# A two-layer encoder step on one core: one phase for load and index projection, feed-forward credits given early, level correction and masks inside the first attention

## The chip, the cores and the metric

The kernel runs on one core of a Trainium2 chip. The metric is the time of one execution in device microseconds (us), as the median of several runs. Before the change it is 3289.69 us (three runs, 3287.46 to 3293.42). The engines are called PE (TensorE, matmul), ACT (ScalarE), DVE (VectorE), POOL (GpSimd) and SP (SyncE, which issues all DMAs here).

## The reference

One inference step over 1024 prompt tokens and 32 sample tokens of width 1024, all in float32. Layer 0 has sparse attention: an index projection gives 8 heads of index queries, one index key and 8 weights per token; their relu scores choose, for each query, the 256 best keys (40 for a sample query), and 16 heads attend to those alone.

```python
dots  = einsum('bthd,bsd->bths', qi, ki)
score = einsum('bths,bth->bts', relu(dots), wi * IDX_SCALE)
score = where(key_pos < chunk_limit(q_pos), score, -inf)
_, sel = top_k(score, n_sel)                 # then softmax attention on k[sel], v[sel], with ALiBi
```

Layer 1 has differential attention. Behind each token mixer stand a residual with layer norm, and then

```python
ffn = (silu(x @ w_gate13) * (x @ w_up13)) @ w2
ple = sigmoid(x @ w_gate) * (p @ w_ple)
y   = layer_norm(ALPHA * x + ffn + ple, g, b)
```

## The kernel before

The program is written by hand, engine by engine. Each phase is a function that returns five streams of instructions, for SP, POOL, PE, ACT and DVE; the streams of all phases are strung together, and semaphores order them. PE, ACT and DVE each go through a barrier (`phase_over`) at the end of some phases; SP and POOL have none and run ahead as far as their own waits let them. Nothing but the written order decides what an engine does next.

Every float32 product of the projections is made of three matmuls: activations are kept as `x_hi` and `x_lo`, weights as `w_hi` and `w_lo`, and hi·hi, lo·hi and hi·lo are added in PSUM. A weight unit is 1024 by 128 (eight 128 by 128 blocks, 512 KB). SP loads it into a slot of a ring (`load_unit`), POOL makes hi and lo of it (`split_unit`, L121 and L123), and PE multiplies it by three pieces of 352 tokens (`unit_product`, L152), 24 matmuls per piece.

**Load (`load_x`, L171).** Eight token tiles of 128 rows come through a buffer of two tiles, `x_nat`. SP loads a tile, PE transposes it in eight blocks (L223), ACT copies each half bank to `x_hi` (L243), DVE subtracts for `x_lo` (L261), and when the transposes of a tile are done SP loads the next into its place. The 32 sample tokens come last (L228). Then DVE makes the row of parameters (L267, L269), the table of distances (L273) and lambda (L278 to L284), and a barrier ends the phase. The weights of the index projection are issued by SP behind all tiles (L107).

**Index projection (`index_projection`, L294).** Five units, 15 pieces; ACT copies each piece out of PSUM (L347, L350); DVE copies the keys (L360); PE transposes keys and weights back to rows (L339); DVE copies these (L362 to L364) and SP stores them. The barrier at the end also waits until that store has landed.

**First attention (`mixer_a`, L374).** It scores all query tiles. Then a search by bits finds for tiles 2 to 7 the level that leaves 256 keys: 31 rounds of counting, tiles 2 to 5 on DVE (L828), tiles 6 and 7 on ACT (L735), while PE works through the projections of q, k and v. Behind the search DVE corrects the levels of tiles 6 and 7 (L848 to L862, two counts at L854), makes the mask of tile 2 in eight operations (`masking`, L874 to L902), and then starts the attention. The attention has 72 steps, eight (two heads each) per query tile, tile 0 first and the sample tile last. In step g PE transposes probabilities of step g-2 (L594), makes the logits of step g (L579), and multiplies for step g-2 (L613); DVE copies a group of transposed probabilities (L943), reads the logits of two heads with the mask added (L929), and scales outputs at every second step (L950, L952); ACT does the exponentials. After the second read of a step DVE does one piece of the mask of the tile that comes three tiles later:

```python
            if g % 8 == 0 and g < STEPS:
                t = g // 8
                later = masking(t + 3) if t + 3 < QT else mask_sample() if t + 3 == SAMPLE else None
```

**Feed-forward (`ffn_norm`, L1755), once per layer.** First the per-layer embedding: eight times a gate (ACT, sigmoid, L2164) and a product, which DVE multiplies into the gate (L2267) and adds with both halves of x into `o_col` (L2270, L2273). Then a loop over pairs of blocks: gate (PE L152, ACT silu L2183), up (DVE L2286), down (L2033, DVE L2257). The waits inside that loop are written as if a round had gone before; so each engine adds credits to its own semaphore once (`s_si` 3, `s_h` 3, `s_hl` 3, `s_da` 24). In the kernel before, ACT gives `s_si` after the last addition of the embedding (L2176, behind a wait on `s_acc`), and DVE gives the others behind its own last instruction of the embedding (L2275 to L2277). PE waits ahead of the loop for the last product into the gate (`s_t`), and in it for `s_da` and `s_si`.

## Time and profile before

| | |
|---|---|
| median of three runs | 3289.69 us |
| the profiled execution | 3293.85 us |
| its span (first to last instruction) | 3292.1 us |
| PE busy | 3108.2 us (94%) |
| PE weight load, DVE, ACT, POOL busy | 2902.7, 1554.4, 887.2, 1021.8 us |
| granted TensorE clock, mean | 0.964 |
| DMA, mean over the span | 45 GB/s |

A matmul row of the timeline gives start and length in us; a group row gives the start of its first instruction. In brackets stand the idle time of the engine before the row and what ended it. PEclk is the granted clock of TensorE as a share of 2.4 GHz: 1.00 is 2.4 GHz, 0.50 is 1.2 GHz. Matmuls are pipelined, so that the time between two starts is shorter than the length of one.

### The profile page before, as it was taken

The page shows a single profiled execution, that of the slowest core. Times are in us where ns is not written, and L with a number is a line of the kernel's source. Part 1 is how long each engine was busy: PE and PEld are TensorE (multiplying, and loading weights), DVE is VectorE, ACT ScalarE, POOL GpSimd, SP SyncE. Part 2 cuts the span into 40 slices and gives each one's busy share as a digit, 9 for nine tenths or more (in the row PEclk, how much of TensorE's full clock was granted, in tenths as well). Part 3 has the DMA queues.
Part 4 walks back from the last instruction along what each step waited for, and adds up shares of the span by engine and source line. Part 5 has one row for each costly group of instructions (what it writes and reads, how often), then busy time and mean ns, then how long its engine had stood idle before and what let it go on. Part 6 is the DMA issues. An engine that isn't in the chain of part 4 may idle for free.

```text
span 3292.1 us, 49272 instructions
## 1 busy us (share of the span) xinstructions
PE 3108.2 (94%) x19621; PEld 2902.7 (88%) x19621; DVE 1554.4 (47%) x2889; ACT 887.2 (27%) x1921; POOL 1021.8 (31%) x495
## 2 busy tenths in 40 slices
PE   7897899989989999999999999998998999999996
PEld 7587677777989999999988999976798999999996
DVE  2589675444544333343363555565454433334335
ACT  2356354434110011100133445454401011110112
POOL 2123000024543343333333222212445343333432
PEclk8998599989999999999999999998999999999998
DMA  2121000012221111111012111111222111111101
GB/s 84 32 53 52 0 1 1 1 52 65 66 83 45 38 51 45 50 45 38 26 46 70 49 42 48 49 40 58 65 85 59 45 45 51 45 45 45 45 7 53
DMA packets 209371, 149.73 MB, mean 45 GB/s; under 512 B 28914, under 2 KB 195764, under 8 KB 209236
## 3 DMA queue, kind: packets, MB, share of 16 engines
q1 hardware_dynamic: 209236, 147.85, 15.1%
q8 instruction: 95, 1.56, 0.2%
q14 instruction: 40, 0.33, 0.0%
HBM read 128.09 MB, written 19.73 MB: 45 GB/s over the span
## 4 chain that ended last, share of the span: by engine, by line
PE 88%; DVE 6%; issue 2%; ACT 2%; POOL 1%; DMA 1%; POOLq 0%; SPq 0%; ACTq 0%; DVEq 0%
PE psum L152 48%; PE psum L2033 15%; PE psum L1637 6%; PE psum L613 5%; PE psum L579 3%; PE psum L594 3%; DVE junk L828 2%; PE psum L1225 2%; PE psum L1199 2%; PE psum L1213 1%; PE psum L534 1%; PE psum L548 1%; PE psum L1174 0%; PE psum L1591 0%; DMA x_nat<-in_x_prompt_dram 0%
## 5 line engine op out<-in xcount | busy, mean ns | idle before, releaser
L152 PE MATMUL psum<-x_hi,w_hi 128*128 128x352 f32 (+1 forms) x3192 | 1041.4, 326 | 40.1 <-ACTq L2176 23.2
L152 PE MATMUL psum<-x_lo,w_hi 128*128 128x352 f32 (+1 forms) x3192 | 1028.0, 322 | 0.0
L152 PE MATMUL psum<-x_hi,w_lo 128*128 128x352 f32 (+1 forms) x3192 | 1027.9, 322 | 0.0
L121 POOL TENSOR_TENSOR w_hi<-w_raw,zeros 128x1024 fp32r<-128x1024 f32 (+1 forms) x209 | 381.9, 1827 | 1549.6 <-PE psum L152 957.8
L152 PEld LDWEIGHTS psum<-x_hi,w_hi 128*128 128x128 f32 (+1 forms) x3192 | 601.7, 189 | 42.8 <-ACTq L2176 23.8
L152 PEld LDWEIGHTS psum<-x_lo,w_hi 128*128 128x128 f32 (+1 forms) x3192 | 602.8, 189 | 0.5
L152 PEld LDWEIGHTS psum<-x_hi,w_lo 128*128 128x128 f32 (+1 forms) x3192 | 601.5, 188 | 0.5
L123 POOL TENSOR_TENSOR w_lo<-w_raw,w_hi 128x1024 fp32r<-128x1024 f32 (+1 forms) x209 | 491.8, 2353 | 16.4
L2286 DVE TENSOR_TENSOR gate<-psum,gate 128x352 f32<-128x352 f32 x120 | 63.0, 525 | 756.9 <-PE psum L152 756.9
L2033 PE MATMUL psum<-h_hi,w_hi 128*128 128x352 f32 x1056 | 340.8, 323 | 1.3 <-DVE h_lo L2308 1.0
L2033 PE MATMUL psum<-h_lo,w_hi 128*128 128x352 f32 x1056 | 338.3, 320 | 0.0
L2033 PE MATMUL psum<-h_hi,w_lo 128*128 128x352 f32 x1056 | 338.1, 320 | 0.0
L2257 DVE TENSOR_TENSOR o_col<-psum,o_col 128x352 f32<-128x352 f32 x528 | 263.3, 520 | 157.4 <-PE psum L2033 155.2
L2033 PEld LDWEIGHTS psum<-h_hi,w_hi 128*128 128x128 f32 x1056 | 198.0, 188 | 2.0 <-issue 1.6
L2033 PEld LDWEIGHTS psum<-h_lo,w_hi 128*128 128x128 f32 x1056 | 198.3, 188 | 0.0
L2033 PEld LDWEIGHTS psum<-h_hi,w_lo 128*128 128x128 f32 x1056 | 197.9, 187 | 0.0
L2290 DVE TENSOR_TENSOR h_lo<-gate,h_hi 128x352 fp32r<-128x352 f32 x120 | 197.3, 1670 | 0.0
L613 PEld LDWEIGHTS psum<-valsA,ptA 128*128 128x128 f32 (+1 forms) x1216 | 154.3, 199 | 40.1 <-issue 25.6
L2186 ACT ACTIVATE h_hi<-gate 128x352 fp32r<-128x352 f32 x120 | 59.8, 498 | 426.9 <-DVE gate L2286 426.9
L613 PE MATMUL psum<-valsA,ptA 128*128 128x65 f32 (+1 forms) x1216 | 172.9, 288 | 0.9 <-ACT ptA L699 0.4
L2183 ACT ACT_TABLE_LOAD x20 | 25.7, 1283 | 499.3 <-PE psum L152 499.3
L1410 DVE CUSTOM_DVE_ANT_0 probB<-psum,distB 128x128 f32<-128x128 f32 (+5 forms) x144 | 96.4, 707 | 121.0 <-PE psum L1199 120.0
(465 smaller groups left out, 4157.0 us busy)
## 6 DMA issues: line engine op xcount, KB each, us to landing
w_raw<-in_ffn_w_dram SPq DMA_DIRECT2D x132, 512.0 KB
w_raw<-in_b_w_in_dram SPq DMA_DIRECT2D x24, 512.0 KB
w_raw<-in_ple_w_gate_dram SPq DMA_DIRECT2D x16, 512.0 KB
x_nat<-in_x_prompt_dram SPq DMA_DIRECT2D x8, 512.0 KB, 3.8
w_raw<-in_a_w_in_dram SPq DMA_DIRECT2D x8, 512.0 KB
w_raw<-in_a_w_in_dram SPq DMA_DIRECT2D x16, 256.0 KB
x_rows<-x_rows SPq DMA_DIRECT2D x8, 512.0 KB, 2.6
out_new_b_v_prompt_dram<-valsB SPq DMA_DIRECT2D x8, 512.0 KB, 3.4
```

What stands on the lines that cost most here:

```text
L121: nc.gpsimd.tensor_tensor(c.w_hi[s][:, 0:kc], c.w_raw[s][:, 0:kc], zero, ALU.add).then_inc(c.split[s], 1)
L123: nc.gpsimd.tensor_tensor(c.w_lo[s][:, 0:kc], c.w_raw[s][:, 0:kc], c.w_hi[s][:, 0:kc].bitcast(F32), ALU.subtract).then_inc(c.split[s], 1)
L152: last = c.nc.tensor.matmul(out, w, x, start=(n == 0), stop=(n == 3 * len(terms) - 1))
L579: mm = nc.tensor.matmul(c.psum[0:n, 1024 * m + a:1024 * m + a + size], queries[rows, 4 * c2 + 2 * i + j, q:q + n], keys[rows, c2, key:key ...
L594: mm = nc.tensor.transpose(bank(c, 4 + k % 2)[0:size, P * x:P * x + n], prob[0:n, g % 3, m, key:key + size], c.ident[0:n, 0:n])
L613: mm = nc.tensor.matmul(c.psum[0:n, at:at + 65], pt[0:size, k, x, 0:n], vals[0:size, blk, 2 * c2 + m, :], start=(j == 0 and x == 0), stop= ...
L828: nc.vector.tensor_scalar(junk[t][:, :], score(t), level[:, t - 2:t - 1], 0.0, ALU.is_ge, ALU.add, accum_out=count[:, t - 2:t - 1]).then_i ...
L1410: nc.vector.tensor_tensor_reduce(prob[:, sl, m, 0:L], c.psum[:, 1024 * m:1024 * m + L], dist[:, o:o + L], slope(h), -LOWEST, ALU.add, ALU.min,
L1637: mm = nc.tensor.matmul(out, o[t % 2][:, u, 0:n], ww[:, cols], start=(j == 0 and x == 0), stop=(j == KC - 1 and x == 2))
L2033: mm = nc.tensor.matmul(o, w[s][:, m, :], h[:, j, piece(t)], start=(j == 0 and k == 0), stop=(j == 1 and k == 2))
L2257: nc.vector.tensor_tensor(o, src, o, ALU.add).then_inc(s_da, 1)
L2290: nc.vector.tensor_tensor(h_lo[:, j, piece(done)], gate[:, 1, piece(done)], h_hi[:, j, piece(done)].bitcast(F32), ALU.subtract).then_inc(s ...
```

## The change

There are three parts.

1. `load_x` and `index_projection` become one phase, `load_index`. All nine token tiles have a place of their own, so SP issues every load without waiting: tiles 0 to 2, weight unit 0, tiles 3 to 5, unit 1, tiles 6 to 8, the parameters, then the other units. PE transposes tiles 0 to 3, multiplies piece 0 of unit 0, transposes tiles 4 and 5, multiplies piece 1, transposes tiles 6 to 8, multiplies piece 2, and goes on with the twelve pieces of units 1 to 4. There is no barrier between the two halves. The parameters are transposed behind the last piece, and DVE copies them there.
2. In `ffn_norm` the credits are given at the start of ACT's and DVE's streams.
3. In `mixer_a` the correction of the levels (`settle`) and the mask of tile 2 move behind the first reads of the attention. The mask of tile t is made during tile t-2, where it was t-3, and two pieces go behind each step, where it was one; `settle` follows the mask of tile 4, in tile 2. Its counts write to `tie`, no longer to `junk`.

```diff
-def load_x(c):
...
+def load_index(c):
+    nat = c.at("x_nat", [P, QT + 1, D], F32, 0)
...
+    GROUP = (0, 1, 1, 2, 2, 2, 3, 3, 3)
+    RING = (4, 5, 6, 7)
...
+    def half_bank(t, b):
+        n = rows(t)
+        return bank(c, RING[(2 * t + b) % 4], 4 * n).rearrange("p (k t) -> p k t", k=4)
...
+        x_tile(0)
+        x_tile(1)
+        x_tile(2)
+        weights(0)
+        for t in (3, 4, 5):
+            x_tile(t)
+        weights(1)
+        for t in (6, 7, 8):
+            x_tile(t)
...
+        def turn_x(t):
+            n = rows(t)
+            pe.wait_ge(s_x[GROUP[t]], 16 * GROUP.count(GROUP[t]))
+            for b in (0, 1):
+                if t >= 2:
+                    pe.wait_ge(s_lo, 2 * t + b - 3)
+                for k in range(4):
+                    mm = nc.tensor.transpose(half_bank(t, b)[:, k], nat[0:n, t, P * (4 * b + k):P * (4 * b + k) + P],
+                                             c.ident[0:n, 0:n])
+                mm.then_inc(s_t, 1)
...
+            if u == 0:
+                pe.wait_ge(s_lo, (6, 12, 18)[t])
...
+        for t in range(4):
+            turn_x(t)
+        project(0, 0)
+        turn_x(4)
+        turn_x(5)
+        project(0, 1)
+        for t in (6, 7, 8):
+            turn_x(t)
+        project(0, 2)
+        for u in range(1, 5):
             for t in range(PIECES):
...
+                project(u, t)
+        pe.wait_ge(s_par, 80)
+        nc.tensor.transpose(bank(c, 6)[:, 0:66], par[:, :], c.ident[0:66, 0:66]).then_inc(s_t, 1)
         pe.wait_ge(s_ca, 16)
         pe.wait_ge(s_q, 12)
         nc.tensor.transpose(c.psum[0:64, 512 * 3:512 * 3 + P], cache[:, :], c.ident[:, :]).then_inc(s_nt, 1)
         pe.wait_ge(s_kw, 3)
+        pe.wait_ge(s_lo, 19)
...
     def vector(v):
...
+        v.wait_ge(s_t, 19)
+        nc.vector.tensor_copy(c.params[:, :], bank(c, 6, 66)).then_inc(s_lo, 1)
+        v.wait_ge(s_lo, 19)
+        nc.vector.tensor_scalar(c.rms_gain[:, :], c.params[:, 64:65], 1.0 - LAMBDA_INIT, None,
+                                ALU.mult).then_inc(s_lo, 1)
         for t in range(PIECES):
             v.wait_ge(s_kw, t + 1)
...
+        def settle():
+            nonlocal masks
+            a = slice(ND, 6)
+            v.wait_ge(s_mask, masks)
+            nc.vector.tensor_scalar(above[:, a], level[:, a], 1.25 * 2.0 ** -24, None, ALU.mult).then_inc(s_mask, 1)
...
+            for t in ON_ACT:
+                v.wait_ge(s_mask, masks)
+                nc.vector.tensor_scalar(tie[:, 0:keys_of(t)], score(t), above[:, t - 2:t - 1], 0.0, ALU.is_ge,
+                                        ALU.add, accum_out=count[:, t - 2:t - 1]).then_inc(s_mask, 1)
+                masks += 1
+                yield
...
-        for _ in masking(2):
-            pass
-        later = None
+        later = ()
         for g in range(STEPS + 3):
             if g % 8 == 0 and g < STEPS:
                 t = g // 8
-                later = masking(t + 3) if t + 3 < QT else mask_sample() if t + 3 == SAMPLE else None
+                for _ in later:
+                    pass
+                if t + 2 <= SAMPLE:
+                    later = itertools.chain(masking(t + 2) if t + 2 < QT else mask_sample(), settle() if t == 2 else ())
...
             if g < STEPS:
                 read_logits(g, 1)
-                if later is not None:
-                    next(later, None)
+                for _ in itertools.islice(later, 2):
+                    pass
...
@@ ffn_norm, scalar
+        act.sem_inc(s_si, 3)
         for x in range(4):
             p_high(x)
...
         act.wait_ge(s_acc, b_acc + 3 * KC)
-        act.sem_inc(s_si, 3)
...
@@ ffn_norm, vector
+        v.sem_inc(s_h, 3)
+        v.sem_inc(s_hl, 3)
+        v.sem_inc(s_da, 24)
         for x in range(5):
             p_low(x)
...
-        v.sem_inc(s_h, 3)
-        v.sem_inc(s_hl, 3)
-        v.sem_inc(s_da, 24)
```

How the change moves DVE's instructions is shown at two places. The line numbers of the changed kernel differ by some lines. The first place is DVE's stream from the last half of x to the rows of the index keys; `kiw` holds the projected keys and weights, `params` the parameters. Before:

```order
L264 TENSOR_TENSOR x_lo<-psum,x_hi 128x8x32
L267 COPY params<-psum 128x66
L269 TENSOR_SCALAR rms_gain<-params 128x1
L273 SCALAR_TENSOR_TENSOR dist<-dist 128x1024
L278 ISA lam_prod,lam_sum<-lam_rows 128x64
```

And with the change:

```order
L349 TENSOR_TENSOR x_lo<-psum,x_hi 128x4x32 x2
L352 SCALAR_TENSOR_TENSOR dist<-dist 128x1024
L356 ISA lam_prod,lam_sum<-lam_rows 128x64
L356 ISA lam_sum 128x1
L356 ISA lam_prod,lam_sum<-lam_rows 128x64
L356 ISA lam_sum 128x1
L360 COPY params<-psum 128x66
L362 TENSOR_SCALAR rms_gain<-params 128x1
L367 COPY ki<-kiw 64x352 x6
L369 COPY kiw_nat<-psum 128x504
```

The copy of the parameters now stands ahead of all six copies of the keys, and it waits for a transpose that PE makes behind the last piece. The second place is DVE's stream from the end of the search into the first steps of the attention. Before:

```order
L845 SCALAR_TENSOR_TENSOR levelA<-levelA 128x6
L848 TENSOR_SCALAR aboveA<-levelA 128x2
L850 TENSOR_TENSOR aboveA<-aboveA,levelA 128x2
L854 TENSOR_SCALAR junk_99,countA<-bias,aboveA 128x896
L854 TENSOR_SCALAR junk_100,countA<-bias,aboveA 128x1024
L858 TENSOR_TENSOR missedA<-countA,wantedA 128x2
L860 TENSOR_TENSOR aboveA<-aboveA,missedA 128x2
L862 TENSOR_TENSOR levelA<-aboveA,levelA 128x2
L874 TENSOR_SCALAR bias<-bias,levelA,signA 128x384
L878 TENSOR_SCALAR tieA,countA<-bias 128x384
```

And with the change:

```order
L857 SCALAR_TENSOR_TENSOR levelA<-levelA 128x6
L950 ISA probA,lowestA<-psum,bias 128x128
L950 ISA lowestA 128x1
L950 ISA probA,lowestA<-psum,bias 128x128
L950 ISA lowestA 128x1
L895 TENSOR_SCALAR bias<-bias,levelA,signA 128x384
L899 TENSOR_SCALAR tieA,countA<-bias 128x384
L950 ISA probA,lowestA<-psum,bias 128x128
```

The first read of logits (L950 in the changed kernel, L929 before) now follows the search at once, and the first two operations of the mask of tile 2 stand behind the second read.

## Rows read from the trace of the kernel before

**Rows 1.** Waits of PE in the whole span: us in total, times, longest

```profile
PE psum L579 <- DVE lowestA L929: 23.4, 1, 23.4
PE psum L152 <- ACTq L2176: 23.2, 2, 11.6
```

**Rows 2.** Windows: start:end, us, busy per engine (instructions), PEclk, DMA share, GB/s

```profile
2.00:4.00 2.00, 0.00 (x0) 0.00 (x0) 0.27 (x5) 0.00 (x0) 0.50 (x1) 1.00 0.91 332
...
341.20:399.40 58.20, 58.15 (x237) 41.69 (x237) 33.52 (x122) 22.81 (x60) 0.00 (x0) 0.50 0.00 1
402.00:418.00 16.00, 15.97 (x118) 11.85 (x116) 13.98 (x36) 9.06 (x18) 0.00 (x0) 1.00 0.01 1
```

**Rows 3.** Timeline of PE in the load phase: start, length, what

```profile
15.76 1.09 PE L223 MATMUL psum<-ident,x_nat 128*128 128x128 f32 x8 [1.67 <-DMA x_nat<-in_x_prompt_dram]
18.43 1.97 PE L223 MATMUL psum<-ident,x_nat 128*128 128x128 f32 x8 [1.58 <-DMA x_nat<-in_x_prompt_dram]
```

**Rows 4.** Timeline of POOL: the split of the first weight unit

```profile
27.66 1.89 POOL L121 TENSOR_TENSOR w_hi<-w_raw,zeros 128x1024 fp32r<-128x1024 f32 x1 [25.16 <-DMA w_raw<-in_a_w_in_dram]
29.63 3.20 POOL L123 TENSOR_TENSOR w_lo<-w_raw,w_hi 128x1024 fp32r<-128x1024 f32 x1
```

**Rows 5.** Timeline of ACT: a half of x, and the first two pieces

```profile
19.67 0.60 ACT L243 ACTIVATE x_hi<-psum 128x512 f32 x1 [0.77 <-PE psum L223]
...
43.26 0.47 ACT L347 ACTIVATE qi<-psum 128x352 f32<-128x352 f32 x1 [8.25 <-PE psum L152]
47.08 0.47 ACT L347 ACTIVATE qi<-psum 128x352 f32<-128x352 f32 x1 [3.35 <-PE psum L152]
```

**Rows 6.** Timeline of DVE: a half of x, the parameters

```profile
21.27 0.69 DVE L261 TENSOR_TENSOR x_lo<-psum,x_hi 128x512 f32 x1 [0.16 <-ACT x_hi L243]
...
27.74 0.21 DVE L267 COPY params<-psum 128x66 f32<-128x66 f32 x1
```

**Rows 7.** The chain that ended last, the first load and the projection

```profile
0.74 3.74 DMA x_nat<-in_x_prompt_dram
...
37.41 59.38 PE psum L152 x360
```

**Rows 8.** Timeline of all engines behind the projection

```profile
97.31 0.70 DVE L360 COPY ki<-kiw 64x352 f32<-64x352 f32 x2 [3.15 <-ACT kiw L350]
...
98.15 0.68 DVE L362 COPY kiw_nat<-psum 128x504 f32<-128x504 f32 x1
...
102.12 3.50 PE L534 MATMUL psum<-ki,qi 64*128 64x512 f32 x8 [4.00 <-DMA t_new_a_kidx_sample_dram<-kiw_nat]
```

**Rows 9.** Timeline of DVE: the end of the first layer's embedding

```profile
937.52 0.51 DVE L2267 TENSOR_TENSOR gate<-psum,gate 128x352 f32<-128x352 f32 x1
...
939.77 2.55 DVE L2273 SCALAR_TENSOR_TENSOR o_col<-x_hi,o_col 128x352 f32<-128x352 f32 x1
```

**Rows 10.** Timeline of PE at the same place

```profile
942.41 0.66 PE L152 MATMUL psum<-x_hi,w_hi 128*128 128x352 f32 x1 [11.60 <-ACTq L2176]
```

**Rows 11.** Timeline of DVE from the level correction to the first read

```profile
333.02 0.17 DVE L848 TENSOR_SCALAR aboveA<-levelA 128x2 f32<-128x2 f32 x1
...
340.67 0.28 DVE L929 CUSTOM_DVE_ANT_0 probA<-psum,bias 128x128 f32<-128x128 f32 x1
```

**Rows 12.** Timeline of DVE: a step of query tile 3 and the start of the next

```profile
421.98 0.69 DVE L929 CUSTOM_DVE_ANT_0 probA<-psum,bias 128x512 f32<-128x512 f32 x1 [0.54 <-PE psum L579]
...
423.21 1.08 DVE L878 TENSOR_SCALAR_CACHE_REDUCE tieA<-bias 128x896 bf16<-128x896 f32 x1
...
425.40 0.69 DVE L929 CUSTOM_DVE_ANT_0 probA<-psum,bias 128x512 f32<-128x512 f32 x1
```

**Rows 13.** Groups of DVE by form in the attention: busy us, mean ns | idle before

```profile
L888 DVE TENSOR_TENSOR_SCAN rankA<-tieA 128x768 int16<-128x768 bf16 x1 | 1.8, 1753 | 0.0
...
L854 DVE TENSOR_SCALAR_CACHE_REDUCE junk<-bias,aboveA 128x1024 bf16<-128x1024 f32 x1 | 1.3, 1275 | 0.0
...
L882 DVE TENSOR_SCALAR tieA<-bias 128x768 bf16<-128x768 f32 x1 | 0.6, 555 | 0.0
```

More of the change, by code:

```diff
@@ L1 @@
+import itertools
 import math
@@ L290 @@
-A_BLOCKS = {"keys": 19072, "vals": 28544, "v_col": 38944, "rows": 43168, "small": 47264, "shared": 47776}
-def index_projection(c):
-    nc = c.nc
+    nat = c.at("x_nat", [P, QT + 1, D], F32, 0)
+    par = c.at("ln_rows", [66, P], F32, 36864)
+    lam = c.at("lam_rows", [P, 4 * 64], F32, 37376)
+    lamp = c.at("lam_prod", [P, 64], F32, 38400)
+    lsum = c.at("lam_sum", [P, 4], F32, 38656)
     base = A_BLOCKS["shared"]
@@ L301, in index_projection @@
     c.qi, c.ki = qi, ki
+    s_x = [c.sem(f"x_loaded{j}") for j in range(4)]
+    s_par = c.sem("params_loaded")
+    s_t, s_hi, s_lo = c.sem("x_transposed"), c.sem("x_hi_done"), c.sem("x_lo_done")
+    s_c, s_l = c.sem("const_steps"), c.sem("lambda_steps")
     s_p, s_q, s_k = c.sem("idx_pieces"), c.sem("idx_queries_copied"), c.sem("idx_keys_copied")
@@ L318, in pool @@
     def pool(g):
+        nc.gpsimd.memset(c.zeros[:, :], 0.0).then_inc(s_c, 1)
+        nc.gpsimd.memset(c.ident[:, :], 0.0).then_inc(s_c, 1)
+        nc.gpsimd.memset(c.eps[:, :], EPS).then_inc(s_c, 1)
+        for s in range(SLOTS):
+            g.sem_inc(c.split[s], 2)
+        g.wait_ge(s_c, 3)
+        nc.gpsimd.affine_select(out=c.ident[:, :], in_=c.ident[:, :], compare_op=ALU.not_equal, fill=1.0,
+                                base=0, pattern=[[-1, P]], channel_multiplier=1).then_inc(s_c, 1)
+        nc.gpsimd.iota(c.dist[:, :], pattern=[[-1, SEQ]], base=SEQ - P, channel_multiplier=1,
+                       allow_small_or_imprecise_dtypes=True).then_inc(s_c, 1)
         for u in range(5):
@@ L343, in scalar, with x_high, drain @@
     def scalar(act):
-        for u in range(4):
-            for t in range(PIECES):
-                await_piece(c, act, "index", 0, u, t, s_p, u)
-                nc.scalar.activation(qi[:, u, piece(t)], bank(c, 3 * (u % 2) + t, TP), ACT.Copy).then_inc(s_q, 1)
-        for t in range(PIECES):
-            await_piece(c, act, "index", 0, 4, t, s_p, 4)
-            nc.scalar.activation(kw[:, piece(t)], c.psum[0:72, 512 * t:512 * t + TP], ACT.Copy).then_inc(s_kw, 1)
+        def x_high(t):
+            for b in (0, 1):
+                act.wait_ge(s_t, 2 * t + b + 1)
+                nc.scalar.activation(c.x_hi[:, 4 * b:4 * b + 4, tokens(t)], half_bank(t, b), ACT.Copy).then_inc(s_hi, 1)
+        def drain(u, t):
+            await_piece(c, act, "index", 0, u, t, s_p, u)
+            if u < 4:
+                nc.scalar.activation(qi[:, u, piece(t)], bank(c, 3 * (u % 2) + t, TP), ACT.Copy).then_inc(s_q, 1)
+            else:
+                nc.scalar.activation(kw[:, piece(t)], c.psum[0:72, 512 * t:512 * t + TP], ACT.Copy).then_inc(s_kw, 1)
+        for t in range(6):
+            x_high(t)
+        drain(0, 0)
+        for t in (6, 7, 8):
+            x_high(t)
+        drain(0, 1)
+        drain(0, 2)
+        for u in range(1, 5):
+            for t in range(PIECES):
+                drain(u, t)
         act.wait_ge(s_nt, 1)
@@ L856, in vector @@
[L856 to L864 removed]
+                                       op1=ALU.mult).then_inc(s_mask, 1)
```

227 lines of the change are left out of this document (80 added, 147 removed).

## The prediction

> **What bounds the kernel now.** I read the waits of PE first, since PE is busy 94% of the span: what counts is where it stands still. [rows 1] name two of the places that the change touches. PE waits once 23.4 us for DVE's first read of logits in the first attention, and twice 11.6 us for one instruction of ACT, the credit of the feed-forward part (L2176). The third place is the start: in the chain of waits the first load takes 3.74 us from 0.74, and the projection's matmuls begin only at 37.41 and last 59.38 us, to 96.79 [rows 7]. At all three places PE has nothing to do, so what is taken off the chain ahead of PE comes off the time, unless another wait ends there.
>
> Then I read the clock in the windows [rows 2]: from 341.2 to 399.4 us, with PE busy 58.15 of 58.20 us, the granted clock is 0.50, which is 1.2 GHz; from 402 to 418 it is 1.00.
>
> **Part 1, the load.** In the window from 2 to 4 us the DMAs move 332 GB/s [rows 2]; a tile or a weight unit of 0.524 MB then takes 1.6 us once the loads stand in a row. The first tile lands at 4.5 us as now. Tiles 1 and 2 follow at 6.1 and 7.6, weight unit 0 at 9.2, tiles 3 to 5 at 10.8, 12.4 and 13.9, unit 1 at 15.5, tiles 6 and 7 at 17.1 and 18.7, the sample rows at 19.1. POOL takes 1.89 + 3.20 us for a unit [rows 4], so unit 0 is split at 14.3 and unit 1 at about 21. PE turns tile 3 only when tile 5 is in, since the three share a semaphore: from 13.9 to 15.9, at 1.97 us a tile at the lower clock [rows 3]. So the first piece starts at 15.9. The first piece of the projection took 43.26 - 37.41 = 5.85 us, the next 3.82 [rows 5]; the first includes the stretch at 1.2 GHz. So it ends at 21.8.
>
> From here I bound from both sides. Behind the last transpose of a group come ACT's 0.60 us and DVE's 0.69 us [rows 5, 6] and some hand-overs, 1.5 us together, in which PE waits. If the clock stays low in each gap, a tile takes 1.97 us and each first piece 5.85: 21.8 + 3.9 + 1.5 = 27.2, 33.0 behind piece 1, plus 4.9 for tiles 6 to 8 (the sample rows taken as half a tile) and 1.5 = 39.5, and 45.3 behind piece 2. If it stays high, a tile takes 1.09 us [rows 3] and a piece 3.82: 25.5, 29.3, 33.5, 37.3. Twelve pieces of 3.82 follow, 45.8 us: the end is at 91.1 or at 83.1, where it was 96.79. I take the middle, **9.7 us** gained, because in the kernel before transposes ran at both clocks within 3 us of each other [rows 3]. What hid the loads before was nothing; now PE's own transposes hide them. SP issues all in a row and stands behind the ring of weights as before.
>
> This is paid for at the end. The copy of the parameters (0.21 us, [rows 6]) now waits for a transpose behind the last piece, and all six copies of the index keys are queued behind it on DVE, where two of the three pairs ran under matmuls. A pair takes 0.70 us [rows 8]. Before, the copy of the rows (L362) started at 98.15, 1.36 us behind the last matmul. Now it is transpose, copy, scaling and hand-overs, some 0.9 us, plus 3 x 0.70 = 3.0 us. PE's first index scores at 102.12 wait for the store that hangs on that copy [rows 8], so they come **1.7 us** later; 1.4 (four copies alone) and 2.3 are the bounds. Lambda's last two steps follow there too, but they lie under the store's 3 us. The old table of distances and lambda's reductions, which held the barrier before the first piece, now run under matmuls. Part 1: 9.7 - 1.7 = **8.0 us**, between 3.4 and 12.3.
>
> **Part 2, the credits.** PE needs three things at the loop: the last product into the gate, DVE's credit and ACT's. The product ends at 937.52 + 0.51 = 938.03, the last addition at 939.77 + 2.55 = 942.32 [rows 9], and PE starts at 942.41 [rows 10], because ACT's credit waits for the addition. With the credits given early the product alone holds PE: it starts at about 938.1, **4.3 us** earlier. Its first weights are there: POOL had split both first units before. ACT's first silu waits for the additions (942.32) and for a piece that ends at 938.1 + 5.85 = 943.9, so it loses nothing. The same wait stands in both layers: **8.6 us**. Should PE keep the high clock through the shorter gap, 2 us more are gained each time; the lower bound is 7, if the start of the loop takes longer than a hand-over.
>
> **Part 3, the first attention.** From the first correction (333.02) to the first read (340.67) DVE works 7.65 us, all of it ahead of PE's wait [rows 11]. This goes: **7.65 us**. But the work itself stays, in steps that are short. In tile 3 a step takes 425.40 - 421.98 = 3.42 us with a mask piece of 1.08 + 0.08 in it, and no idle time before the next read [rows 12]: the rest of DVE's work is 2.26 us. That step now gets pieces 3 and 4 of a mask of 768 keys, 0.56 + 0.15 + 1.75 = 2.46 us [rows 13], the 0.15 being an estimate for a one-column operation: 4.7 us, **1.3 us** more. The like happens once per tile: some 0.6 in tiles 0 and 1, 1.1 in tile 2 where both counts of the correction, 1.27 and a little less, fall in one step, 1.5 and 1.7 in tiles 4 and 5, whose masks are longer. That is 6.8 us in all if nothing gives, and 0 if PE's queued work bridges it. I take 5, nearer to the first, since the row shows no idle time. Part 3: 7.65 - 5 = **2.7 us**, between 0.9 and 7.65.
>
> Weighed against the clock's row: rows 2 show 58 us of busy PE at 1.2 GHz, and the same number of matmuls would take 237 x 16.0 / 118 = 32 us at the rate of the next window. I let this stretch stand as it is and move it as a whole. The Trainium skill, "TensorE: Matmul & The Clock Gate", Part 1, says that the low clock is the state at rest and that sustained matmul activity releases it. By that rule the stretch should hardly exist, and the trace does not agree. If the rule held in the changed kernel, up to 26 us more would be gained.
>
> **The sum.** 8.0 + 8.6 + 2.7 = 19.3 us. The profiled execution took 3293.85 us (span 3292.1), 4.2 above the median shown; less 19.3 it would be 3274.6, and the median of the runs becomes 3289.69 - 19.3 = **3270.4 us**. What a measurement here can tell from no change is about 0.2%, 6.6 us.
>
> **The rivals.**
> *Low clock in the load, and full stalls.* The clock is low in every gap of the load and DVE's pairs stall to the full: 3.4 + 7 + 0.9, a gain of 11, 3278. For it: the clock fell while PE turned tiles [rows 3]. Chance 0.14.
> *The clock rises earlier in the attention.* PE now rests some 16 us where it was 23.4, and the stretch at 1.2 GHz may be shorter. A third of it at the higher rate saves 9 us: gain 28 to 30, 3261. Against it: PE was busy throughout the stretch and the clock stayed low. Chance 0.12. This is also where the skill's rule leads.
> *The credits give nothing.* The next wait in the loop, DVE's product behind ACT's silu, ends as late as now, and Part 2 is lost: gain 10.7, 3279. For it: DVE's additions still end at 942.32. Against it: DVE's first product needs a piece of the second unit, 8 us later. Chance 0.05.
> *Slower: the low clock lasts longer.* The stalls of DVE make the matmuls of tiles 2 and 3 sparser, and the clock does not come back at tile 2. A matmul costs 0.246 us there and 0.136 at the high rate [rows 2], so 100 matmuls cost 11 us. With some 175 more of them at the low clock the gain is gone, and from about 235 the kernel is slower by more than can be missed; through tiles 2 and 3, about 360 matmuls, it is 40 us more and 3310. Against it: at 1.2 GHz the steps are longer and DVE has time. Chance 0.04.
> *Several terms give way at once* and less than 6.6 us is left, 3285: 0.05.
>
> **How the numbers follow.** The forecast has 0.60. It, the first three rivals, all on the faster side, make 0.91; no change 0.05; slower 0.04. The range leaves out the slower case, the weakest one and the far ends: down to 3257 (the early clock with the load's upper bound), up to 3283.
>
> **What would show it.** The first product matmul at 16 us and the last of the projection between 83 and 91; the wait for ACT's credit gone and PE idle about 7.3 us there, ended by DVE's product (L2267 before); the wait for the first read 16 us, not 23.4; DVE without idle time in the second step of tiles 2 to 5; the clock at 1.00 again some 58 us after the first step. I am wrong if the projection ends later than 91, if the gap at the loop stays over 10 us, or if the clock comes back in another tile.

## The result, and the profile after

| | before | changed |
|---|---|---|
| median of four runs, side by side | 3291.48 us | 3262.01 us |
| lowest to highest | 3287.46 to 3293.42 | 3254.72 to 3265.27 |
| the profiled execution (its span) | 3293.85 (3292.1) | 3254.72 (3252.9) |
| PE busy | 3108.2 us | 3091.2 us (95%) |
| granted TensorE clock, mean | 0.964 | 0.973 |

The ratio is 0.9907, with a 95% interval from 0.9892 to 0.9921: the change saves 29.5 us (26.0 to 35.5 by the interval), where 19.3 was forecast. A second measurement beside other runs of before, e5 below, gave 0.9923 [0.9903, 0.9942], 24.2 us by the medians. The profiled execution of the changed kernel was the fastest of its four, and that of the kernel before (3293.85) was slower than all of its four, so the two profiles differ by 39.2 us of span. The difference must be read place by place.

**Where PE waits.** The waits of PE in the changed kernel (columns as in [rows 1]):

```profile
PE psum L591 <- DVE lowestA L950: 15.7, 1, 15.7
PE psum L153 <- DVE gate L2291: 15.3, 2, 7.7
...
PE psum L267 <- DMA x_nat<-in_x_prompt_dram: 8.0, 3, 4.5
...
PE psum L546 <- DMA t_new_a_kidx_sample_dram<-kiw_nat: 5.3, 1, 5.3
```

The wait for the first read of logits fell from 23.4 to 15.7 us. The wait for ACT's credit is gone. In its place stands the wait for the last product into the gate, 7.7 us twice where it was 11.6.

**The load.** The chain of waits up to the end of the projection (start us, us, what):

```profile
4.26 9.32 DMA x_nat<-in_x_prompt_dram
13.62 1.10 PE psum L267 x8
14.72 3.82 PE psum L153 x24
18.54 0.45 PE psum L267 x4
19.01 0.61 ACT x_hi L315
19.64 2.50 DVE x_lo L349 x4
22.27 5.64 PE psum L153 x24
27.91 0.45 PE psum L267 x4
28.38 0.61 ACT x_hi L315
29.01 2.89 DVE x_lo L349 x6
32.04 51.51 PE psum L153 x312
```

In this chain the first product starts at 14.72 (14.48 by PE's timeline), where it was 37.41 [rows 7], and the last matmul ends at 83.55, where it was 96.79: 13.2 us earlier. Between the first two pieces, and between the second and the third, the chain goes over ACT's and DVE's halves of x; PE stands still there for 1.99 and 1.25 us. The windows around these stops (columns as in [rows 2]):

```profile
14.40:18.40 4.00, 4.00 (x28) 3.98 (x27) 1.29 (x2) 1.01 (x2) 2.91 (x2) 1.00 1.09 302
18.40:22.20 3.80, 1.89 (x17) 1.65 (x15) 2.48 (x4) 2.42 (x5) 1.37 (x1) 1.00 0.78 181
22.20:27.70 5.50, 5.43 (x24) 5.46 (x25) 0.00 (x0) 0.00 (x0) 0.00 (x0) 0.69 0.14 42
27.70:32.00 4.30, 2.79 (x26) 2.34 (x24) 2.99 (x7) 2.87 (x7) 0.00 (x0) 1.00 0.00 0
32.00:36.00 4.00, 3.96 (x15) 3.99 (x16) 1.40 (x5) 0.00 (x0) 0.00 (x0) 0.58 0.00 0
```

Each stop is followed by a stretch in which the granted clock fell to 0.50 (means of 0.69 and 0.58 over these windows), although PE was busy in it. The stops thus cost more than their own length: piece 1 took 5.64 us and piece 0 took 3.82. Two waits of PE ahead of them, 1.51 us before 8.00 and 1.94 us before 13.62, were not followed by such a fall: the granted clock was 1.00 up to 22.4.

**Behind the projection.** The timelines of DVE and PE there (compare [rows 8]):

```profile
83.72 0.23 DVE L360 COPY params<-psum 128x66 f32<-128x66 f32 x1 [50.28 <-PE psum L298]
...
84.06 2.17 DVE L367 COPY ki<-kiw 64x352 f32<-64x352 f32 x6
86.25 0.68 DVE L369 COPY kiw_nat<-psum 128x504 f32<-128x504 f32 x1
...
90.21 1.23 PE L546 MATMUL psum<-ki,qi 64*128 64x512 f32 x2 [5.32 <-DMA t_new_a_kidx_sample_dram<-kiw_nat]
```

The copy of the rows starts 2.70 us behind the last matmul, where it was 1.36. The first index scores start at 90.21, 11.9 us before the old 102.12.

**The first read.** DVE's timeline at the end of the search:

```profile
321.19 0.17 DVE L857 SCALAR_TENSOR_TENSOR levelA<-levelA 128x6 f32<-128x6 f32 x1
321.33 0.29 DVE L950 CUSTOM_DVE_ANT_0 probA<-psum,bias 128x128 f32<-128x128 f32 x1
```

The read comes at 321.33, where it was 340.67 [rows 11]: 19.3 us earlier, 11.9 from the load and 7.4 from the correction and the mask that no longer stand ahead of it.

**The loop of the feed-forward part.** PE's timeline in the first layer (compare [rows 10]), and DVE's in the following fence (compare [rows 9]):

```profile
907.40 0.66 PE L153 MATMUL psum<-x_hi,w_hi 128*128 128x352 f32 x1 [7.67 <-DVE gate L2291]
```

```profile
906.45 0.51 DVE L2291 TENSOR_TENSOR gate<-psum,gate 128x352 f32<-128x352 f32 x1
906.99 1.67 DVE L2294 SCALAR_TENSOR_TENSOR o_col<-x_lo,gate 128x352 f32<-128x352 f32 x1
```

PE starts 0.44 us behind the end of the last product, while the two additions behind it are not done.

**The attention.** Windows of the changed kernel from the first read on:

```profile
321.20:350.00 28.80, 27.99 (x116) 19.81 (x116) 19.24 (x80) 12.34 (x36) 0.00 (x0) 0.50 0.00 1
352.00:368.00 16.00, 15.56 (x114) 11.23 (x110) 12.42 (x44) 9.25 (x22) 0.00 (x0) 1.00 0.01 2
```

The low clock lasts 28.7 us behind the first read, where it lasted 58.7 [rows 2]. The first read of tile 1 comes 18.4 us behind the first of all, as before (18.0), but that of tile 2 at 40.4 (before 49.3) and that of tile 3 at 66.0 (before 77.9). From there to the last tile the distance stays between 11.2 and 11.9. The first matmul that takes the attention's output comes at 665.93, where it was 697.40.

So the 39.2 us between the two profiles are: load and projection 11.9, first read 7.4, the attention itself 12.2 (31.5 less 19.3), and the two feed-forward loops 3.5 and 4.1: PE starts the first at 907.40, where it was 942.41, 35.0 us earlier, and the second at 2459.49, where it was 2498.62, 39.1 earlier. The attention's 12.2 is the part that the forecast had only as a rival.

### The profile page after: what moved, and what is told of

Same layout as the page of the kernel before. It is cut to its first block, busy times and chain, and to the rows that moved or that the text cites. A ratio compares the mean times of both kernels' runs of the same rounds, so it can differ in the third digit from the quotient of the medians.

```text
span 3252.9 us, 49145 instructions
## 1 busy us (share of the span) xinstructions
PE 3091.2 (95%) x19621; PEld 2890.8 (89%) x19621; DVE 1544.2 (47%) x2890; ACT 883.0 (27%) x1919; POOL 1021.4 (31%) x495
## 4 chain that ended last, share of the span: by engine, by line
PE 88%; DVE 7%; issue 2%; ACT 2%; POOL 1%; DMA 1%; SPq 0%; POOLq 0%; ACTq 0%; DVEq 0%
PE psum L153 48%; PE psum L2054 16%; PE psum L1658 6%; PE psum L625 4%; PE psum L591 2%; PE psum L606 2%; DVE junk L840 2%; PE psum L1246 2%; PE psum L1220 2%; PE psum L1234 1%; PE psum L546 1%; PE psum L560 1%; PE psum L1195 0%; PE psum L1612 0%; PE psum L1857 0%
## 5 line engine op out<-in xcount | busy, mean ns | idle before, releaser
L153 PE MATMUL psum<-x_hi,w_hi 128*128 128x352 f32 (+1 forms) x3192 | 1041.7, 326 | 25.3 <-DVE gate L2291 15.3
```

The costliest lines, as they stand in the source:

```text
L153: last = c.nc.tensor.matmul(out, w, x, start=(n == 0), stop=(n == 3 * len(terms) - 1))
```

## The experiments

TensorE's clock in the first attention is named often below; "return" is the time from the first read of logits to the moment at which the granted clock goes back to 1.00, in the profiled execution. Three kernels make one part of the change each:

**e1_load_only.** The old kernel with the new phase alone (`load_index` in place of `load_x` and `index_projection`):

```diff
-def load_x(c):
...
-def index_projection(c):
+def load_index(c):
```

> Part 1 of the change alone. Theory (the parts add up): PE's first index scores start 11 to 12 us earlier than in the kernel before (102.1 there, 90.2 in the changed kernel), the gain is 11 to 12 us, the wait for the first read of logits stays 23.4 us, and the clock in the attention rises some 58 us after the first read, as before. Rival (the clock's rise hangs on the moment at which the phases fall, not on the rest before the attention): with the same rest of 23.4 us the rise comes at another distance from the first read, by 10 us or more, and the gain is that much off 12.

**e2_credits_only.** The old kernel with the credits at the start of the streams:

```diff
@@ ffn_norm, scalar
+        act.sem_inc(s_si, 3)
...
-        act.sem_inc(s_si, 3)
@@ ffn_norm, vector
+        v.sem_inc(s_h, 3)
+        v.sem_inc(s_hl, 3)
+        v.sem_inc(s_da, 24)
...
-        v.sem_inc(s_h, 3)
-        v.sem_inc(s_hl, 3)
-        v.sem_inc(s_da, 24)
```

> Part 2 of the change alone. Theory: PE's gap ahead of each feed-forward loop falls from 11.6 to 7.7 us, 3.9 us each, 7.8 us together, ended by DVE's product into the gate. Rival (the next wait in the loop gives it back): the gap shrinks but the loops' ends move by less than 2 us each and the time by less than 4.

**e3_attention_only.** The old kernel with the new order of correction and masks:

```diff
-        for _ in masking(2):
-            pass
-        later = None
+        later = ()
...
+                for _ in itertools.islice(later, 2):
+                    pass
```

> Part 3 of the change alone. Theory: the first read of logits comes 7.4 us earlier, the doubled mask pieces cost 5 to 7 us in tiles 0 to 5, and the rest of the gain is the clock: it rises between 25 and 58 us after the first read, so the gain lies between 1 and 13 us and differs from run to run. Rival (the earlier rise in the changed kernel came from the shift by Part 1): the clock rises 58 us after the first read as before, and the gain is 0 to 3 us in every run.

Measured, beside 25 runs of before (median 3284.21, 3280.33 to 3300.64):

| | runs | median | ratio | saved us |
|---|---|---|---|---|
| e1 | 10 | 3281.11 | 0.9975 [0.9961, 0.9990] | 8.2 [3.3, 12.8] |
| e2 | 10 | 3276.45 | 0.9973 [0.9957, 0.9989] | 8.9 [3.6, 14.1] |
| e3 | 10 | 3283.44 | 0.9988 [0.9972, 1.0003] | 3.9 [-1.0, 9.2] |

The savings follow from the ratios, which rest on all runs; the medians alone differ by 3.1, 7.8 and 0.8 us. The three together make 21.0 us by the ratios and 11.6 by the medians, so the totals bear out the order of size and no more. The waits of PE in e1, e2 and e3, one fence each:

```profile
PE psum L589 <- DVE lowestA L939: 23.4, 1, 23.4
PE psum L152 <- ACTq L2186: 23.2, 2, 11.6
```

```profile
PE psum L579 <- DVE lowestA L929: 23.4, 1, 23.4
PE psum L152 <- DVE gate L2270: 15.4, 2, 7.8
```

```profile
PE psum L153 <- ACTq L2187: 23.2, 2, 11.6
PE psum L581 <- DVE lowestA L940: 15.7, 1, 15.7
```

Each part takes away its own wait and leaves the others as they were, so the parts are independent there. In e1 the index scores start at 89.51, 12.6 us earlier, and all of it is still there at the first read (328.21, 12.5 earlier). In e2 the loop starts 4.0 us earlier in the first layer (938.37 for 942.41) and 6.3 in all by the second (2492.33 for 2498.62). In e3 the first read comes at 333.58, 7.1 earlier.

The clock in the attention is where they differ. One window of e1 and one of e3:

```profile
329.00:386.00 57.00, 56.98 (x234) 41.39 (x236) 33.26 (x122) 22.55 (x59) 0.00 (x0) 0.50 0.00 1
```

```profile
334.00:378.00 44.00, 43.75 (x182) 32.07 (x184) 25.18 (x102) 18.10 (x50) 0.00 (x0) 0.50 0.00 0
```

In e1 and e2 the return is 58.8 us, as in the kernel before. In e3 it is 45.3, and in the whole change 28.7. In the profiled executions Part 3 thus brings an earlier return, and the other two alone don't. That it is so in all executions is not shown: the profiled one of e2 was the longest of its ten (3288.23, mean clock 0.968), and its shortest took 3272.23 us at a mean clock of 0.974; e1's profiled one had 0.965, and three of its ten took 3270.58 to 3275.86 us at 0.970.

**e4_warm.** Does the shorter rest of PE ahead of the first read decide the return? The changed kernel, with 100 matmuls whose result nobody reads, so that PE rests 8.6 us ahead of the first read and not 15.7:

```diff
+        for _ in range(100):
+            nc.tensor.matmul(c.psum[:, 512 * 3:512 * 3 + TP], c.x_hi[:, 0, 0:P], c.x_hi[:, 0, 0:TP], start=True, stop=True)
         pe.wait_ge(s_drained, 36)
```

> The changed kernel with 100 matmuls of 352 columns added on PE behind the last projection, in PE's rest of 24 us ahead of the attention; their result goes to a PSUM bank that nothing reads. They take 16 us at 2.4 GHz. Theory (a clock that has fallen needs long to come back in the light matmuls of tiles 0 and 1, but one that is still high stays): PE rests some 8 us instead of 24; if the clock is 1.00 at the first read or soon after, tiles 0 and 1 take some 25 us instead of 40 and the kernel gains 8 to 12 us over the changed one. Rival (the light matmuls of tiles 0 and 1 don't hold the high clock at all): the clock falls again within the first tile, and the gain is under 3 us.

Measured 3265.28 us (3263.83 to 3268.58, 4 runs), 0.9938 [0.9913, 0.9962]. The clock fell at 316.6 with the first read at 320.12, and returned 54.5 us behind it:

```profile
321.00:374.00 53.00, 52.89 (x218) 38.04 (x216) 29.44 (x115) 20.89 (x56) 0.00 (x0) 0.50 0.00 1
```

A shorter rest alone does not bring an earlier return. The kernel was no faster for it.

**e5_change_again.** The changed kernel once more, to see how much of the return is chance.

> The changed kernel as it is, on the chip of the other runs of this call. Theory (parts plus a clock that comes back at different moments): 20 to 30 us faster than the kernel before, with a spread of some 10 us between runs. If the first measurement of 29.5 us was made by luck in the clock, the gain here is nearer to 20.

Measured 3260.77 us (3251.61 to 3266.62, 6 runs) beside 3285.01 of before (11 runs): 0.9923 [0.9903, 0.9942]. The return was 28.9 us, where it was 28.7, and the first reads of tiles 1 to 3 came at 18.4, 40.5 and 66.1 us behind the first of all, within 0.1 us of the other profile. In the profiled executions it is stable. Of the unprofiled ones only the mean clock is on record: in the first measurement 0.970, 0.971 and 0.970 against 0.973 in the profiled one, which was 5 to 11 us faster, and in e5 between 0.968 (3266.62 us) and 0.975 (3251.61 us). By these means executions of the same program differ by 13 to 20 us at 1.2 GHz in the first measurement and by up to 46 in e5 (an estimate: twice the difference of the means, times the span of some 3255 us); where in the span is not seen.

**e6_one_piece.** One piece of a mask per step as before, and the four pieces of `settle` behind the masks of the first four tiles:

```diff
+        settling = settle()
...
-                    later = itertools.chain(masking(t + 2) if t + 2 < QT else mask_sample(), settle() if t == 2 else ())
+                    later = itertools.chain(masking(t + 2) if t + 2 < QT else mask_sample(),
+                                            itertools.islice(settling, 1) if t < 4 else ())
...
-                for _ in itertools.islice(later, 2):
+                for _ in itertools.islice(later, 1):
```

> The changed kernel with one mask piece behind each step, as before the change, and the four pieces of the level correction as the eighth piece of tiles 0 to 3. Theory (from the tiles' times: tile 3 took 31.6 us against 30.9, tiles 4 and 5 the same, tile 0 18.4 against 18.0): the doubled pieces cost 1 to 1.5 us in all, so this kernel is at most 1.5 us faster than the changed one at the same clock, with tile 3 back at 30.9. Rival (the prediction's term): the doubled pieces cost 5 us, and this kernel is 4 to 5 us faster.

Measured 3263.50 us (3250.22 to 3269.06, 6 runs), 0.9922 [0.9903, 0.9940]: no difference to e5. Tile 0 took 18.1 us and tile 3 30.8 where the changed kernel takes 18.4 and 31.6; tile 4 took 43.2 in both. But the return came only after 63.0 us in the profiled execution, the longest of the six, so this run does not price the doubled pieces in tiles 1 and 2; e11 below does.

**e7_warm140.** As e4 with 140 matmuls, so that PE comes to the first logits at the full clock without a rest. (Only the number in e4's edit differs.)

> The changed kernel with 140 added matmuls of 352 columns instead of 100: 22.4 us at 2.4 GHz, from 296.9 to 319.3, so PE doesn't rest before the first read at 321. With 100 the clock fell at 316.6, 3.5 us before the first read. Theory (a clock still high is kept by the attention): the clock is 1.00 through tiles 0 and 1, these take some 35 us together instead of 49 (tiles 0 and 1 after the first read), and the kernel is 5 to 14 us faster than the changed one. Rival (the light matmuls don't hold it): the clock falls within tile 0 and the gain is under 3 us.

Measured 3260.93 us (3259.13 to 3271.53, 6 runs), 0.9929 [0.9912, 0.9946]. Windows of its profile:

```profile
316.00:323.00 7.00, 5.57 (x37) 5.16 (x35) 6.71 (x23) 4.03 (x8) 0.00 (x0) 1.00 0.00 1
327.00:360.00 33.00, 33.00 (x138) 23.84 (x137) 18.91 (x74) 13.56 (x38) 0.00 (x0) 0.50 0.00 1
362.00:378.00 16.00, 15.07 (x109) 11.10 (x110) 13.77 (x42) 8.87 (x21) 0.00 (x0) 1.00 0.00 1
```

The clock was 1.00 up to 3.4 us behind the first read, fell at 326.5, and stayed at 0.50 although PE was busy 33.00 of the 33.00 us from 327. So the low clock of tile 0 does not need the long rest ahead of it. But PE was not busy all the time before this fall. Its timeline there:

```profile
323.73 0.49 PE L591 MATMUL psum<-keysA,o_col 64*128 64x128 f32 x4 [2.16 <-DVE lowestA L952]
...
325.14 0.49 PE L591 MATMUL psum<-keysA,o_col 64*128 64x128 f32 x4 [0.55 <-DVE lowestA L952]
...
326.65 0.69 PE L625 MATMUL psum<-valsA,ptA 128*128 128x65 f32 x2 [0.65 <-DVE ptA L966]
```

In the 5 us ahead of the fall PE had stood 2.16 and 0.55 us, and it fell within the third stop of 0.65. What is shown is that the attention's matmuls did not bring the clock back for 34 us with PE always busy; whether they alone would have lost it is not.

**e8_load_order.** The load phase with fewer stops: PE turns tiles 0 to 5, multiplies piece 0, turns 6 to 8, and multiplies pieces 1 and 2; the parameters are transposed there and not behind the last piece:

```diff
-        for t in range(4):
+        for t in range(6):
             turn_x(t)
         project(0, 0)
-        turn_x(4)
-        turn_x(5)
-        project(0, 1)
         for t in (6, 7, 8):
             turn_x(t)
+        project(0, 1)
         project(0, 2)
+        pe.wait_ge(s_par, 80)
+        nc.tensor.transpose(bank(c, 6)[:, 0:66], par[:, :], c.ident[0:66, 0:66]).then_inc(s_t, 1)
```

> The changed kernel with PE's order in the load as tiles 0 to 5, piece 0, tiles 6 to 8, pieces 1 and 2, and with the parameters' transpose behind piece 2 of unit 0 instead of behind the last piece. Theory: the two waits for x_lo between products (1.99 and 1.25 us) go, the copies of the first four index keys go under matmuls again; the last matmul of the projection ends 1 to 5 us earlier than 83.6, the first index scores follow 4.8 us behind it instead of 6.6, and the kernel is 3 to 6 us faster than the changed one. Rival (PE then waits as long ahead of piece 0 for the tiles' loads and for DVE): the end of the projection stays within 1 us of 83.6, and only the 1.7 us of the copies is gained.

Measured 3258.77 us (3249.79 to 3260.5, 6 runs), 0.9907 [0.9890, 0.9924], 2.0 us under e5 with intervals that overlap. In the profile the product starts later (18.07 in the chain), but the last matmul ends at 78.67, 4.9 us before the changed kernel's, and the index scores start at 83.96, 6.3 us before. Of this a part was lost again in the attention, where the return took 54.2 us:

```profile
316.00:369.00 53.00, 52.88 (x218) 38.05 (x218) 29.46 (x115) 20.90 (x56) 0.00 (x0) 0.50 0.00 1
```

**e9_hold.** e8's load, e7's 140 matmuls, and four matmuls without a reader in each step of tile 0, so that PE has more work there; the last of these edits:

```diff
             if g < STEPS:
                 logits(g)
+            for _ in range(4 if g < 8 else 0):
+                nc.tensor.matmul(c.psum[:, 512 * 3:512 * 3 + TP], c.x_hi[:, 0, 0:P], c.x_hi[:, 0, 0:TP], start=True, stop=True)
```

> The kernel with the other load order, with the 140 added matmuls ahead of the attention, and with four more of 352 columns behind the logits of each of the eight steps of tile 0. Theory (what tile 0 lacked in e7, where the clock fell 3.3 us after the first read, is matmul work; tile 1 holds a clock that is already high, as tiles 2 on do): the clock is 1.00 from the first read on, tile 0 stays near 18 us, tile 1 takes 18 to 20 us where it took 22 to 31, and the first two tiles take some 37 us together against 40.5 to 49.6; the gain over e8 is 3 to 12 us, and the runs spread less. Rival (the clock falls in tile 1 all the same): tiles 0 and 1 take over 44 us.

Measured 3244.83 us (3243.72 to 3247.35, 4 runs), 0.9871 [0.9854, 0.9888]. A window of its profile around the end of tile 0:

```profile
314.00:328.00 14.00, 13.97 (x100) 11.55 (x96) 9.67 (x49) 6.96 (x23) 0.00 (x0) 1.00 0.01 1
```

The clock stayed at 1.00 from 191.8 to 635.5 us. PE waited there too for the first read of logits, but once and 1.3 us, where e7 had 2.16, 0.55 and 0.65; so the added matmuls also shorten PE's rests, and the two are not told apart. The first reads of tiles 1 to 3 came 15.6, 34.7 and 60.3 us behind the first of all. The runs spread over 3.6 us; those of the changed kernel spread over 15 in e5.

**e10_hold_only.** e9 without the 140 matmuls ahead of the attention: the load of e8 and the four per step.

> As e9, but without the 140 matmuls ahead of the attention: the clock is low at the first read. Theory (the added matmuls of tile 0 make it dense enough): the clock rises within tile 0, and tiles 0 and 1 take 37 to 42 us. Rival (at the low clock four more matmuls per step only lengthen the step, some 1.2 us each): tile 0 takes 25 us or more, and the kernel is slower than e8.

Measured 3251.17 us (3247.68 to 3271.16, 5 runs), 0.9886 [0.9868, 0.9903]. The profiled execution was the longest of the five. Its windows:

```profile
296.00:338.00 42.00, 24.83 (x99) 20.24 (x100) 28.82 (x109) 19.22 (x44) 0.00 (x0) 0.50 0.04 13
339.00:345.00 6.00, 5.38 (x35) 3.46 (x34) 5.50 (x20) 3.08 (x9) 0.00 (x0) 1.00 0.00 0
346.00:379.00 33.00, 33.00 (x134) 24.02 (x133) 17.22 (x55) 12.31 (x28) 0.00 (x0) 0.50 0.00 1
```

Here the clock came back at the very end of tile 0 (its first read was at 314.88, that of tile 1 25.3 us behind it) and fell again in tile 1, at 345.4, behind a wait of PE of 0.26 us and within one of 0.99. The other four runs, some 19 us and more below it with a mean clock of 0.975 to 0.977 (0.967 in the profiled one), can't have had all of this. The run is inconclusive on the 140 matmuls, and by these clocks one program can go either way.

**e11_hold_one_piece.** e9 with e6's one piece per step.

> As e9 with one mask piece per step and the level correction spread as in e6. Theory: with the clock high DVE bounds tiles 1 and 2 where two pieces fall in one step, so the spread pieces gain 1 to 4 us over e9. Rival (the doubled pieces are absorbed also there): within 1 us of e9 in the tiles' times.

Measured 3241.99 us (3240.72 to 3243.26, 4 runs), 0.9859 [0.9842, 0.9876]. It is the fastest of all: beside 3286.56 of before (9 runs) it is 44.6 us faster, and its slowest run lies under every run of the change. The window from the first read to the end of its attention, and then the like one of the changed kernel:

```profile
316.00:636.00 320.00, 309.45 (x2294) 243.14 (x2294) 199.47 (x529) 156.46 (x276) 0.00 (x0) 1.00 0.00 1
```

```profile
322.00:636.00 314.00, 302.36 (x2120) 234.51 (x2120) 194.65 (x491) 150.22 (x253) 0.00 (x0) 0.96 0.00 1
```

With the clock high in all of it, the doubled pieces can be priced. Tile 1 takes 18.2 us here and 19.1 in e9; tile 2 takes 23.8 and 25.6, and 25.6 in the changed kernel too, whose clock is high by then; tile 3 takes 30.8 and 31.6 (changed kernel 31.6, before 30.9). Tile 4 takes 43.2 in both. So two pieces per step cost 0.9, 1.8, 0.7 and nothing.

**e12_turns_first.** The load phase without any interleaving: PE turns all nine tiles and then multiplies; ACT's stream follows the same order.

```diff
-        for t in range(4):
-            turn_x(t)
-        project(0, 0)
-        turn_x(4)
-        turn_x(5)
-        project(0, 1)
-        for t in (6, 7, 8):
+        for t in range(9):
             turn_x(t)
-        project(0, 2)
+        for t in range(PIECES):
+            project(0, t)
...
```

> The changed kernel with all nine tiles turned before the first product, so nothing is interleaved, but with the loads in a row and without the barrier. Theory (most of the load's gain is the missing wait for loads and the missing chain on DVE, not the interleaving): the first product starts at 22 to 24 us, the projection ends within 2 us of the changed kernel's 83.6, and the time is the same within 2 us. Rival (interleaving is what gains): the projection ends 4 us later or more.

Measured 3263.24 us (3260.16 to 3263.53, 5 runs), 0.9921 [0.9906, 0.9936]. The window of the whole projection:

```profile
21.50:79.00 57.50, 57.50 (x364) 56.13 (x362) 2.69 (x9) 6.78 (x15) 12.86 (x6) 1.00 0.04 9
```

The product starts 7 us later than in the changed kernel, then runs without a stop at the full clock, and ends at 79.1, 4.5 us before it. The index scores start at 85.72, 4.5 us earlier too. So the interleaving of transposes and products, as written, costs time. What the new phase gains comes from the loads that no longer wait for a free place, from weights that are split meanwhile, and from the barrier that is gone. Ahead of it stood DVE's table of distances and lambda, and the kernel before has this row among its waits of PE, which the changed one has not:

```profile
PE psum L152 <- DVEq L2457: 10.2, 1, 10.2
```

How the gain divides among the three was not measured. In the total nothing of the 4.5 us is seen, since the return was 45.1 us here and the medians of e5 and e12 stand beside different runs of before.

**The return in all profiles**, with the time from the first read to the first reads of tiles 2 and 3:

| | return | tile 2 | tile 3 |
|---|---|---|---|
| before, e1, e2 | 58.7, 58.8, 58.8 | 49.3 | 77.9 |
| changed, e5 | 28.7, 28.9 | 40.4, 40.5 | 66.0, 66.1 |
| e7 (fell 3.4 behind the read) | 37.5 | 44.3 | 70.0 |
| e3, e12 | 45.3, 45.1 | 47.8, 47.7 | 73.4 |
| e8, e4 | 54.2, 54.5 | 49.6, 49.7 | 77.4 |
| e6 | 63.0 | 49.3 | 79.8 |
| e10 (fell again in tile 1, back for good at 64.7) | 23.7 | 55.2 | 83.9 |
| e9, e11 (never fell) | | 34.7, 33.7 | 60.3, 57.5 |

The kernels that come to the attention at the low clock sort by the mask pieces: with one per step (before, e1, e2, e6) the return lies between 58.7 and 63.0 us, with two (changed, e3, e4, e5, e8, e12) between 28.7 and 54.5. e5 and e6 differ in how the pieces of masks and correction are spread alone, with the same rest of 15.7 us, and their profiles have 28.9 and 63.0. So it is the pieces inside the steps, not the shorter rest, that go with the earlier return in these profiles; by what way is not shown. (e7, e9, e10 and e11 come to the attention at the high clock or have added matmuls in it.)

## Why the prediction was right or wrong

The side was right, the measured 3262.01 lies in the range, and the forecast was 8.4 us too high. The range was wide enough for this because its lower end counted in an early clock, which the forecast itself had put at nothing. The rows of the changed kernel allow a judgement of each step.

**Part 1, the load: 8.0 forecast, 11.9 measured.** The gain at the last matmul, 13.2, lies between the bounds of 5.7 and 13.7, near the upper one, where the middle of 9.7 was taken. Two things were mis-sized. The loads were faster than the 332 GB/s of [rows 2]: 371, 341, 398 and 389 GB/s in the four windows of 2 us from 4 to 12 us, and the first product started at 14.5, not at 15.9. And the clock fell for two short stretches, not in every gap: piece 0, which both bounds took at 5.85, took 3.82. The loss behind the projection was 13.2 less 11.9, 1.3 us, where 1.7 was forecast: the six copies and the copy of the parameters stand where they were expected, and the six took 2.17 us, 0.07 more than three pairs.

**Part 2, the credits: 8.6 forecast, 7.9 measured** by the two gaps (7.6 by the two starts), and 8.9 [3.6, 14.1] in e2. The gap is 7.67 us, the forecast said about 7.3, and the wait that ends it is the predicted one. The forecast let PE start 0.1 us behind the product; it took 0.44. The rival in which the credits give nothing is out, by e2's total, and because PE waits for nothing else in the first 50 us of the loop. The clock did not stay high through the shorter gap: the first matmul behind it took 0.66 us, as before [rows 10].

**Part 3, the head: 7.65 forecast, 7.4 measured** (7.1 in e3). **The doubled mask pieces: 5 forecast, 2.9 measured** in the changed kernel (0.4 in tile 0, 1.8 in tile 2, 0.7 in tile 3). In tile 1, whose steps are half at the low clock, it lies between nothing (31.3 us in e8, 31.2 in the kernel before, both at the low clock) and 0.9 (e9 and e11, at the high clock). This is the term that failed in size. The sum took it from a step without idle time in [rows 12], as if each microsecond of DVE's were PE's. In tiles 4 and 5, where 3.2 us were expected, there was none: between 418 and 512 us the changed kernel has no wait of PE for DVE. So what DVE loses in one step it makes good before PE runs out of queued work. The forecast named this as the lower end and put its weight near the other. Part 3 is then 4.5 and not 2.7.

**The clock in the attention: 0 forecast, up to 12 in the profiles.** The step that failed reads "I let this stretch stand as it is and move it as a whole". It held in the profiles for Parts 1 and 2 alone (e1, e2: 58.8 us), and not for Part 3. The rival "the clock rises earlier in the attention" described what the profile then showed, with 3261 us for it, and had a chance of 0.12; its reason, the shorter rest, is what e4, e6 and e8 contradict, where the rest was as short or shorter (8.6, 15.7, 15.7 us) and the return late (54.5, 63.0, 54.2). The Trainium skill, "TensorE: Matmul & The Clock Gate", Part 1, says that sustained matmul activity releases the low clock. In this attention the trace does not agree: in e7 PE was busy 33.00 of 33.00 us at 0.50. In e9, with four matmuls of 352 columns more in each step of tile 0, the clock was 1.00 throughout.

Without the clock the measured parts make 11.9 + 7.9 + 4.5 = 24.3 us. The two measurements of the whole gave 29.5 [26.0, 35.5] and 24.2 [19.1, 31.9]. So between nothing and some 5 us of the median may be the clock's (up to 11 by the first interval), and the 12 us of the profile are likely more than a usual run has: the profiled execution had the highest mean clock of its four. That the rest of the miss, 24.3 against 19.3, lies in the load and in the mask pieces is read from the profiles; how often the unprofiled runs had the early return is not shown.

**The rivals on the slow side** did not occur: the projection ended at 83.55, not behind 91, and the clock returned in tile 1 and not behind tile 3.

**What stays open** is what fixes the moment of the return. It moves from 28.7 to 63.0 us with edits that hardly change the matmuls of tiles 0 and 1, is earlier with two mask pieces per step than with one, and repeats within 0.1 us in the two profiles of the same program. It was not tried to shift the first read by a few microseconds with nothing else changed, which would tell whether its place in time decides.

## What to carry to other kernels

Where an engine waits for a credit that another gives behind work it doesn't need, give the credit early and the next true dependence shows at once in the list of waits; this is worth reading off before any larger rewrite. When work is moved into short steps, an idle-free step is no proof that the added time is paid: look whether the waiting engine has queued work of its own, and at which clock its steps run. And read the granted clock beside the busy share: a fully busy PE stood at 1.2 GHz for 29 to 63 us here, and some dense matmuls nobody reads, put where the light ones stand, won some 15 us (from e12 to e9 18.4 by the medians, less the 3.7 us that e9's index scores came sooner); the four runs of e9 lie within 3.6 us, the six of e5 within 15.

## What the runs showed of the hardware

- PE busy for 33.00 of 33.00 us with the attention's small matmuls (138 of them) had a granted clock of 0.50 (e7). It had fallen from 1.00 behind stops of PE of 2.16 and 0.55 us and within one of 0.65, all in 5 us. With 140 dense matmuls ahead and four further ones of 352 columns per step of tile 0 the clock stayed at 1.00 for the 443.7 us from 191.8 to 635.5 (e9).
- The same program has the same return in two profiles (28.7 and 28.9 us), while one kernel, e10, made four runs of 3247.68 to 3252.27 us and one of 3271.16 whose clock went 0.50, 1.00, 0.50 and 1.00 within the first 65 us of the attention.
- Short stops of PE in the load phase (1.99 and 1.25 us) were each followed by a fall of the clock 0.1 to 0.6 us after it had started again, and piece 1 took 5.64 us for 3.82; stops of 1.51 and 1.94 us ahead of them were not. A phase without stops that started 7 us later ended 4.5 us sooner (e12).
